# A decoder block with a mixture of experts: the gather of token rows by f32 products, and a piece of a down weight loaded ahead

## The reference

```python
h = rmsnorm(x, norm_moe_w)                    # (256, 1024)
logits = h @ w_router + b_router              # 32 experts
top_v, top_i = lax.top_k(logits, 4); gates = softmax(top_v)
for each expert e:                            # xb: the rows of h that chose e
    gu = xb @ w_gate_up[e] + b_gate_up[e]     # (., 1024) @ (1024, 2048)
    gate, up = min(gu[:, :1024], 7), clip(gu[:, 1024:], -7, 7)
    act = (up + 1) * gate * sigmoid(1.702 * gate)
    y[rows] += gates * (act @ w_down[e] + b_down[e])   # (., 1024) @ (1024, 1024)
out = rmsnorm(x + y, norm_final_w)
```

## Time and profile before

| | |
|---|---|
| median of 3 runs | 1184.41 us (1184.17 to 1184.76) |
| profiled execution, device time | 1184.76 us |
| its span | 1183.0 us (1.76 us lie around it) |
| mean granted TensorE clock | 0.986 |
| TensorE busy | 1134.4 us, 96% |
| HBM read | 442.55 MB, 375 GB/s over the span |

### The profile page before, as it was taken

One profiled execution on the slowest core, in us unless ns is written; L12 is line 12 of the kernel. 1 busy time (PEld: TensorE's weight loads), 2 busy tenths in 40 slices (PEclk: granted clock), 3 DMA queues, 4 the chain that ended last, 5 costly groups with the idle time before them and its releaser, 6 DMA issues.

```text
span 1183.0 us, 18703 instructions
## 1 busy us (share of the span) xinstructions
PE 1134.4 (96%) x7502; PEld 574.9 (49%) x7503; DVE 381.3 (32%) x891; ACT 181.8 (15%) x395; POOL 22.0 (2%) x65
## 2 busy tenths in 40 slices
PE   9999999999999999999999999999999999999996
PEld 8989889855434444344333333333333333333332
DVE  4988878455221111222211111111111111111112
ACT  4611521343100000000000000000000000000002
POOL 4000010000000000000000000000000000000000
PEclk9999999999999999999999999999999999999999
DMA  9954204989999999999999999999999999999995
GB/s 324 369 172 144 73 10 155 346 330 398 417 428 432 429 431 431 429 433 431 433 430 433 431 430 433 431 431 433 431 433 430 432 432 431 432 432 423 426 424 226
DMA packets 41353, 444.24 MB, mean 376 GB/s; under 512 B 4270, under 2 KB 5656, under 8 KB 24540
## 3 DMA queue, kind: packets, MB, share of 16 engines
q1 hardware_dynamic: 39868, 440.45, 88.9%
q0 software_dynamic: 480, 1.85, 0.6%
q10 hardware_dynamic: 960, 1.31, 0.4%
HBM read 442.55 MB, written 1.05 MB: 375 GB/s over the span
## 4 chain that ended last, share of the span: by engine, by line
PE 67%; DMA 31%; DVE 1%; ACT 0%; SPq 0%; issue 0%; DVEq 0%; ACTq 0%
DMA ring<-in_w_gate_up 30%; PE bank L1180 23%; PE bank L1171 13%; PE bank L736 7%; PE bank L732 4%; PE bank L1210 4%; PE bank L1225 3%; PE bank L875 1%; PE bank L715 1%; PE bank L1107 1%; PE bank L1296 1%; PE bank L1201 1%; PE bank L1287 1%; PE bank L913 1%; PE bank L1019 1%; PE bank L1141 1%
## 5 line engine op out<-in xcount | busy, mean ns | idle before, releaser
L1180 PE MATMUL bank<-ring,region 128*64 128x512 f32 x2048 | 464.0, 608 | 36.0 <-DMA ring<-in_w_gate_up 36.0
L1180 PEld LDWEIGHTS bank<-ring,region 128*64 128x64 f32 x2048 | 147.0, 140 | 333.5 <-issue 268.7
L1171 PE MATMUL bank<-ring,region 128*64 128x512 f32 x1024 | 226.8, 595 | 0.3 <-ACT region L1419 0.3
L2328 DVE TENSOR_SCALAR region<-bank 128x512 f32<-128x512 f32 x32 | 22.1, 691 | 573.9 <-PE bank L1180 573.9
L1171 PEld LDWEIGHTS bank<-ring,region 128*64 128x64 f32 x1024 | 71.1, 137 | 130.1 <-issue 127.2
L1419 ACT ACTIVATE region<-bank 128x256 f32<-128x256 f32 (+1 forms) x130 | 53.4, 437 | 367.0 <-PE bank L1171 251.1
L1419 ACT ACTIVATE bank<-region 128x512 f32<-128x512 f32 x32 | 19.2, 601 | 452.5 <-DVE region L2328 452.5
L736 PE MATMUL bank<-ring 128*128 128x256 f32 x392 | 86.6, 380 | 0.0
L736 PEld LDWEIGHTS bank<-ring 128*128 128x128 f32 x392 | 73.8, 190 | 10.9 <-issue 0.7
L1210 PE MATMUL bank<-region 64*128 64x512 f32 x264 | 65.6, 615 | 0.1
L1225 PEld LDWEIGHTS bank<-region,r_levels 128*128 128x128 bf16 x1536 | 61.3, 118 | 1.6 <-issue 1.6
(11 more groups left out here) (318 smaller groups left out, 774.0 us busy)
## 6 DMA issues: line engine op xcount, KB each, us to landing
ring<-in_w_gate_up SPq DMA_DIRECT2D x48, 4096.0 KB, 30.2
ring<-in_w_down SPq DMA_DIRECT2D x24, 4096.0 KB, 36.5
ring<-in_w_gate_up SPq DMA_DIRECT2D x26, 2048.0 KB, 14.3
ring<-in_w_down SPq DMA_DIRECT2D x10, 2048.0 KB, 13.3
ring<-in_w_in SPq DMA_DIRECT2D x6, 2048.0 KB, 19.8
ring<-in_w_gate_up SPq DMA_DIRECT2D x11, 1024.0 KB, 35.6
ring<-in_w_xkv SPq DMA_DIRECT2D x4, 2048.0 KB, 11.0
ring<-in_w_down SPq DMA_DIRECT2D x7, 1024.0 KB, 8.3
```

The source lines that it names most:

```text
L1171: last = pe.matmul(bk[half * ROWS:(half + 1) * ROWS, :], lhs, w[:, half * 512:(half + 1) * 512], start=start, stop=stop, skip_group_check= ...
L1180: last = pe.matmul(rows, lhs, columns[:, half], start=start, stop=stop, skip_group_check=True)
L2328: v.tensor_scalar(g_t, bank_g[:, :], LIMIT, None, ALU.min).then_inc(sem["g_clamped"], 1)
```

## The change

- `h2` is kept once, in f32 (8 KB a partition of `r_levels`); all of `cut` and `rest` go, and with them 15 copies on ACT and 10 subtractions on DVE.
- The gather is 8 tiles x 2 token halves of f32 products, with the scaled selection as the moving side, and the weights again every fourth column of a row, now f32. `scales`, `keep_warm`, the unscaled selection and the copy `row_scales` go; the multiply `scale_xb` becomes a plain copy `take_rows`.
- The freed 4 KB a partition of `r_levels` (`spare`) take the first quarter (0.5 MB) of chunk (1, 5). It is loaded ahead of chunk (1, 1); the later load of the first half of (1, 5) is that much shorter. TensorE reads this quarter from `spare`.
- The last quarter of chunk (1, 4) is loaded right behind chunk (1, 1), when `x2_squared` reaches 3, not at the end of the parts. For it `half_squares` moves to where the rests lay.
- At the lead the gate's bias product comes ahead of the second half of the gather, and the wait on `rs_ready` goes.

```diff
@@ SP
             load_cols(1, 3, 0, D)
+            sp.wait_ge(sem["x1_squared"], NT)
+            sp.dma_start(spare, source(*SPARE)[:, 0:D]).then_inc(sem["spare_in"], 16)
             wait_full(sp, "xo01")
             load_chunk(1, 1)
+            sp.wait_ge(sem["x2_squared"], 3)
+            load_cols(1, 4, 3 * D, SLOT)
             sp.wait_ge(sem["seeded"], NT)
             load_cols(1, 4, 0, D)
...
             load_cols(1, 4, D, 3 * D)
-            sp.wait_ge(sem["cut_ready"], CUTS * len(PIECES))
-            load_cols(1, 4, 3 * D, SLOT)
...
-                    load_cols(e, k, 0, SLOT // 2)
+                    load_cols(e, k, D if (e, k) == SPARE else 0, SLOT // 2)
@@ TensorE
             def gather(tiles):
                 for k in tiles:
-                    for i in range(3):
-                        for t in range(NT):
-                            last = pe.matmul(bank_a[:, k * ROWS:(k + 1) * ROWS], h2_parts[:, i, t, rows_of(k)], sel[:, t, :],
-                                             start=(i == 0 and t == 0), stop=(i == 2 and t == NT - 1), skip_group_check=True)
+                    for t in range(NT):
+                        last = pe.matmul(bank_a[:, k * ROWS:(k + 1) * ROWS], h2[:, t, rows_of(k)], scaled_sel[:, t, :],
+                                         start=(t == 0), stop=(t == NT - 1), skip_group_check=True)
                 return last
...
-            keep_warm()
-            scales([0])
-            pe.wait_ge(sem["sel_ready"], 1)
-            pe.wait_ge(sem["cut_ready"], 3 * CUTS)
-            gather_half(range(KT // 2), 1)
+            bias_of(bank_g, 0)
             pe.wait_ge(sem["scaled_ready"], 1)
-            scales([1]).then_inc(sem["rs_psum"], 1)
+            pe.wait_ge(sem["xw_ready"], 3)
+            gather_half(range(KT // 2), 1).then_inc(sem["lead_rows"], 1)
...
                     if not final:
-                        next_rows(1)
-                        pe.wait_ge(sem["actT_rest"], w1)
-                        pe.wait_ge(sem["scaled_ready"], pe.snap(w1 + 1))
-                        scales().then_inc(sem["xb_psum"], 1)
+                        next_rows(1).then_inc(sem["xb_psum"], 1)
...
+                            w = wk[:, a * D:(a + 1) * D]
+                            if in_spare and (j, a) == (DOWN_CHUNKS - 1, 0):
+                                pe.wait_ge(sem["spare_in"], 16)
+                                w = spare
@@ DVE
-            def scale_xb(lo, hi, signal):
+            def take_rows(lo, hi, signal):
                 src = bank_a[:, lo * ROWS:hi * ROWS].rearrange("p (k r) -> p k r", r=ROWS)
-                v.tensor_tensor(xbT[:, lo:hi, :], src, row_scales.unsqueeze(1).broadcast_to([P, hi - lo, ROWS]),
-                                ALU.mult).then_inc(signal, 1)
+                v.tensor_copy(xbT[:, lo:hi, :], src).then_inc(signal, 1)
```

More of the change, by code:

```diff
@@ L1184, in bias_of @@
                 pair_of_inner(bk, one_hot, b_gu[:, c0:c0 + D], True, False)
-            def keep_warm():
-                pe.matmul(bank_g[:, 0:T], ident[:, :], iota, start=True, stop=True)
             def gather_half(tiles, t):
                 for k in tiles:
-                    for i in range(3):
-                        last = pe.matmul(bank_a[:, k * ROWS:(k + 1) * ROWS], h2_parts[:, i, t, rows_of(k)], sel[:, t, :],
[L1195 to L1201, removed]
+                    last = pe.matmul(bank_a[:, k * ROWS:(k + 1) * ROWS], h2[:, t, rows_of(k)], scaled_sel[:, t, :],
+                                     start=(t == 0 and k == 0), stop=(t == NT - 1), skip_group_check=True)
                 return last
@@ L1213, in scatter @@
                         last.then_inc(signal, 1)
+                return last
             def rows_of(k):
@@ L1222, in gather @@
                 for k in tiles:
[L1223 to L1226 removed]
+                    for t in range(NT):
+                        last = pe.matmul(bank_a[:, k * ROWS:(k + 1) * ROWS], h2[:, t, rows_of(k)], scaled_sel[:, t, :],
+                                         start=(t == 0), stop=(t == NT - 1), skip_group_check=True)
                 return last
[L1229 removed]
+            pe.wait_ge(sem["xw_ready"], 2)
             gather_half(range(KT), 0)
@@ L1268, in one_time, with expert @@
                 pe.matmul(first_of_psum, first_col, spans, start=True, stop=True).then_inc(sem["blocks_psum"], 1)
-            def expert(e, slots, counts, last_tiles={}, lead=False, final=False, by_halves=False):
+            def expert(e, slots, counts, last_tiles={}, lead=False, final=False, by_halves=False, in_spare=False):
                 def next_rows(half):
-                    pe.wait_ge(sem["sel_ready"], pe.snap(w1 + 1))
-                    gather(range(half * KT // 2, (half + 1) * KT // 2))
+                    pe.wait_ge(sem["scaled_ready"], pe.snap(w1 + 1))
+                    return gather(range(half * KT // 2, (half + 1) * KT // 2))
                 def scatter_and_combine():
@@ L1282, in scatter_and_combine @@
                         pe.wait_ge(sem["gT_ready"], 1)
-                    scatter()
+                    last = scatter()
+                    if final:
+                        last.then_inc(sem["xb_psum"], 1)
                     pe.wait_ge(sem["selg_ready"], w1)
@@ L1385, in expert @@
                         last.then_inc(sem["chunk_used"], 1)
[L1386 to L1389, removed]
+                    if not final:
                         pe.wait_ge(sem["one_hot_ready"], pe.snap(w1 + 1))
@@ L1401, in _ @@
             for e in range(HEAD):
-                expert(e, slots(e), counts(e), lead=(e == 0), by_halves=(e < BY_HALVES))
+                expert(e, slots(e), counts(e), lead=(e == 0), by_halves=(e < BY_HALVES), in_spare=(e == SPARE[0]))
             with pe.Fori(0, TURNS) as i:
@@ L1679, in _ @@
             act.wait_ge(sem["gu_part_ready"], 3)
-            for i in range(CUTS):
-                cut(0, i)
             half_squared(0, 1)
-            for i in range(CUTS):
-                cut(1, i)
             half_squared(1, 0)
[L1686 to L1689, removed]
             seed(0, 0, "xo01")
             seed(0, 1, "eT01")
+            gate_exps(0)
             wait_taken(act, "router0")
@@ L2358, in _ @@
             weigh_rows(0)
-            rest(0, 0)
-            rest(0, 1)
             add_rows("xo", 0, 1)
@@ L2458, in _ @@
                 e, rows = bass.ds(e_of, 1), iota[:, bass.ds(row_of, ROWS)]
-                select(e, rows)
                 select_scaled(e, rows)
```

70 lines of the change are left out of this document (13 added, 57 removed).

## The result

The changed kernel takes **1393.76 us** (1391.5 to 1394.82), the kernel before 1184.29 us: a ratio of 1.176, interval 1.1747 to 1.1775. It is slower by 209 us, where 13 were forecast. The direction was right; the size lies far outside the range of 1190 to 1208.

What follows compares the result with a forecast made beforehand. The prediction took the DMA stream to bound the kernel, with TensorE 3.0 us an expert faster than the transfers. Profiled 1184.76 + 9.0 (stream late) + 4.0 (tail) = 1197.8 us, range 1190 to 1208.

Steps and rivals of the forecast that it cites:

- the margins: At SP's DMA issues: how much later each may come before the stream halts; 0.2, 1.1 and 2.0 us mattered.
- the couple that was named: The 4 MB transfer issued at 462.77 us: margin 2.0 us, and the stream 9.0 us late there.
- 4.2 and more: Issues after 462.77 us: margins of at least 4.2 us, growing by 3 an expert, so no larger delay later.
- The gather's price: Each expert's gather: 32 instructions at 110 ns, 3.52 us, so an expert costs TensorE 1.45 us more.
- the stride is dear: Rival on the gather: 177 ns an instruction, TensorE the bound throughout, 1248 us (1208 at 140 ns); chance 0.12.
- The loads ahead: Early loads for chunks (1, 5) and (1, 4): 1.05 MB or 2.4 us into idle time, costing and gaining nothing.
- The lead: Before expert 0: it starts 0.3 us later, tiles 4 to 7 add 0.5, releases from 286.23 come 0.8 later.
- The tail: Expert 29 to the end: 4.0 us added behind the stream.
- Faster: Rival: only transfers count, TensorE's added time vanishes in waits, 2.4 us saved, 1182.3 us; chance 0.06.
- the stream does not halt: Rival on the DMA stream: the delay is hidden, 9.0 shrinks to 2 or 4, 1190 to 1193 us; chance 0.06.

Runs made afterwards that it cites:

- extra_first: Kernel before plus seven unused f32 products, columns side by side, ahead of the gather's second half in experts 0 to 4: 1192.31 us, ratio 1.0067.
- extra_loop: Kernel before plus seven unused f32 products, columns side by side, ahead of the gather's second half in experts 5 to 28: 1186.37 us, ratio 1.0013.
- side_by_side: Changed kernel with only the layout of h2 altered, so a gather tile's 128 columns lie side by side: 1198.02 us, ratio 1.0108.

## Why the prediction was wrong, step by step

- **What bounds the kernel before, and the margins.** The mechanism was right: extra_first and extra_loop show it, and side_by_side has its halt at the couple that was named. That this couple is 8.8 us late for 9.0 is partly luck. Its issue is 12.0 us later, where 0.8 + 7 x 1.45 = 11.0 was forecast (the lead 2.6 and not 0.8, an expert 1.33 and not 1.45), and the margin was larger than 2.0: 8.6 us wasn't a transfer with empty queues. In side_by_side the 2 MB issued at 288.81 (before 286.23) land in 7.2 us, and the 4 MB couple in 12.3, not 13.5. Going the other way, the next couple's margin wasn't "4.2 and more" but 17.7 - 15.9 = 1.8, so the stream ends up 10.1 to 10.5 us late and not 9.0.
- **The gather's price. This is the step that failed.** "I take 110 ns, because three f32 rows lie there": it is 226 to 233. The shape stood nowhere in the trace, and the bounds were 107 and 177; the upper one wasn't a bound. It was made by adding the 70 ns between two transposes' loads to the spacing of plain ones. The transposes of L1296 at the same step load in 211 ns, the weights of the plain f32 products in 329. What the transpose has that a plain product lacks no run here shows, so its row could carry neither the middle nor the end of the range. The rows on which I rested (the text says three and shows two, L732 and L1124) were of columns side by side: they agreed with each other about another case. With 230 ns in the sum of the rival "the stride is dear", and no clock, 31 gathers x 5.3 us less 53.7 of waits, plus lead and tail, gives some 120 us; the other 85 or so are the clock's.
- **The Trainium skill's rule** (TensorE: Matmul & The Clock Gate, section LDWEIGHTS), a load priced by its columns alone, is right side by side (108 ns an instruction here for its 107) and nearly at 8 bytes (114), and fails for f32 from 12 bytes on (171). The measurement decides. Its other rule, that the fast load isn't for FP32 (section on weight-path perf modes), fits what the change did: the bf16 gather, 8 bytes apart, ran at 33 ns, and f32 at the same distance takes 114.
- **The clock.** No step had it; the prediction left it at full without a reason. It costs 2.46 + 0.29 us an expert, and at the lead the first chunk takes 5.85 us for 3.65. A gather of 7.3 us in which 64 columns move every 230 ns reads as 100% busy, and the clock falls in it all the same.
- **The sum of the changed kernel** closes with these terms: lead +7.5 us (294.52 against 287.01 and what follows them), 31 x 8.0 = 248, less 54 us that the kernel before lost to waits for DMA and to the clock behind them (53.7 by the prediction's sum), +7.4 in expert 31: 208.9 for 208.8 between the spans. The 54 are what makes the account of experts 1 to 30 close, not a number read off.
- **The loads ahead are worth nothing.** Fits (1393.27 for 1393.76, where TensorE was the bound; to about 1 us in the other layout). The reason can be read off the code, though no run shows it by itself: the quarter of slot 0 that (1, 5) no longer fills stays empty, so ring and `spare` together hold no byte more at 286 us than the ring did before. The premise that went with it, a margin of 0.2 us at that issue, was too small: by the 7.2 us above it was 1.6.
- **The lead.** 0.8 us was forecast for side by side; its third chunk starts at 289.67 for 287.08 of before, 2.6 later, 1.7 of it the halved clock.
- **The tail.** 4.0 forecast. From the last shared wait for DMA on, side_by_side loses 1197.0 - 1183.0 - 10.5 = 3.5 us. So the 14.0 us between the spans are 10.5 + 3.5 for 9.0 + 4.0: the stream is sized too low and the tail too high, each by a little. The agreement of 1198.02 with the forecast of 1197.8 is of that kind too.
- **Rivals.** "The stride is dear" was the right mechanism with 0.12 of the chance and too low an end, 1248 us; it had no clock in it either. "Faster" and "the stream does not halt" are excluded by side_by_side and extra_first.

## What to carry to other kernels

An operand's access pattern is part of its price. Before an operand changes its type under a step, look for a row with the same type, the same step and the same kind of instruction; if there is none, the upper end is open and the range has to say so, or the data is laid side by side, which here gave back 196 us. A run of instructions that load much and move few columns can cost twice on TensorE: its own time, and the clock of the dense products behind it (here behind two halves of 3.6 to 3.7 us). And where a DMA stream is the bound, added work on another engine is paid at the issues with the emptiest queues: read issue against landing, not busy shares, and take the landing with empty queues from an issue that surely has them.

## What the hardware showed that was not expected

- Plain f32 products, ns an instruction, by distance of the weight columns: 108, 114, 171, 226 to 233, 231 to 237 ns for 4, 8, 12, 16, 32 bytes; the same at 2.4 and at 1.2 GHz (3.73 and 3.61 us for 16). The weight loads themselves last 192, 196, 261, 329 and 334 ns by the trace. In bf16 8 bytes apart: 33 ns an instruction.
- The clock went from 2.4 to 1.2 GHz for 10.2 us an expert behind two strided halves (3.7 + 3.6 us with 0.85 between), for 3.4 us behind one of 3.7 (from expert 1 on; in expert 0 not), and not at all with halves of 2.7 us or, from expert 1 to 30, pieces of 2.0 between dense products of 3.6.
- In the kernel before, the clock falls to half for 3.4 us eight times between 604 and 1045 us, each time about the end of a wait for DMA, and is 0.986 over the span. extra_loop fills much of these waits with products nobody needs, has no such fall and 0.998, and does 24 x 1.5 us more work for 1.2 us.
